# One block per chunk in the DeltaNet matrices, and a second pair of heads that runs two steps behind

## The reference

```
gcum = cumsum(g);  decay = exp(gcum_i - gcum_j) where i >= j, else 0
a_mat = where(i > j, (k*beta) @ k^T * decay, 0) + I          # 64 x 64
u, w  = solve(a_mat, [v*beta, k*beta*exp(gcum)])             # unit lower triangular
v_new = u - w @ state
o     = (q*exp(gcum)) @ state + ((q @ k^T) * decay) @ v_new
state = state*exp(gcum_end) + (k*exp(gcum_end - gcum))^T @ v_new
```

## Time and profile before

| | us |
|---|---|
| median of 3 runs | 2914.16 |
| these runs | 2910.6, 2914.16, 2915.44 |
| profiled execution's own time | 2922.2 |
| its span, first to last instruction | 2920.4 |

### The profile page before, as it was taken

One profiled execution on the slowest core, in us unless ns is written; L12 is line 12 of the kernel. 1 busy time (PEld: TensorE's weight loads), 2 busy tenths in 40 slices (PEclk: granted clock), 3 DMA queues, 4 the chain that ended last, 5 costly groups with the idle time before them and its releaser, 6 DMA issues.

```text
span 2920.4 us, 37357 instructions
## 1 busy us (share of the span) xinstructions
PE 2310.8 (79%) x12376; PEld 1057.1 (36%) x12376; DVE 2092.9 (72%) x5401; ACT 1428.7 (49%) x4102; POOL 1178.7 (40%) x1032
## 2 busy tenths in 40 slices
PE   9998888787978888788786678667786677678887
PEld 5465433243422443234432333223332333233332
DVE  3857877777777776777766777777766777776664
ACT  4425545564456455454443544444444544444344
POOL 0003444444444434444444444444444444444442
PEclk9999989999988889899987898988988899989999
DMA  7348999999999999999999999999999999999998
GB/s 269 104 168 355 418 410 409 415 411 419 419 419 420 410 389 372 419 420 416 405 406 421 418 416 416 413 421 416 412 404 421 420 416 412 414 421 421 421 421 349
DMA packets 187042, 1148.16 MB, mean 393 GB/s; under 512 B 19808, under 2 KB 40288, under 8 KB 55648
## 3 DMA queue, kind: packets, MB, share of 16 engines
q0 software_dynamic: 147456, 1073.81, 89.2%
q1 hardware_dynamic: 24512, 53.67, 5.1%
q10 hardware_dynamic: 14880, 18.29, 1.7%
HBM read 1132.06 MB, written 13.63 MB: 392 GB/s over the span
## 4 chain that ended last, share of the span: by engine, by line
DMA 38%; PE 32%; DVE 11%; ACT 7%; issue 3%; POOL 3%; ACTq 0%; DVEq 0%; POOLq 0%
DMA ring_mem<-in_experts,work 37%; PE bank L1985 13%; DVE ring_mem L1607 6%; PE bank L1842 4%; PE bank L1641 3%; PE bank L1966 3%; POOL ring_mem L813 3%; PE bank L1802 3%; PE bank L1891 2%; ACT work L1149 1%; DMA kept_tiles<-ring_mem 1%; ACT work L1145 1%; ACT L1145 1%; PE bank L1799 1%; ACT L984 1%
## 5 line engine op out<-in xcount | busy, mean ns | idle before, releaser
L813 POOL DMA_INDIRECT ring_mem<-in_experts,work x1024 | 1178.3, 1151 | 1717.0 <-PE bank L1986 1154.1
L1607 DVE CUSTOM_DVE_ANT_0 ring_mem<-ring_mem,work 128x1024 f32<-128x1024 f32 x1024 | 1251.9, 1223 | 554.1 <-DMA ring_mem<-in_experts,work 544.8
L1985 PE MATMUL bank<-ring_mem,work 64*64 64x512 f32 x3584 | 1022.3, 691 | 352.9 <-ACT work L1149 347.8
L1986 PE MATMUL bank<-ring_mem,work 64*64 64x512 f32 x3584 | 1022.4, 691 | 0.0
L1145 ACT ACTIVATE work<-work 128x1 f32<-128x1 f32 x1024 | 206.3, 202 | 1167.7 <-DVE work L1607 1128.9
L1985 PEld LDWEIGHTS bank<-ring_mem,work 64*64 64x64 f32 x3584 | 247.9, 147 | 885.8 <-ACT work L1149 510.0
L1149 ACT ACTIVATE work<-work 128x64 f32<-128x64 f32 (+1 forms) x1024 | 364.3, 356 | 34.0 <-ACT work L1145 0.2
L1137 ACT ACTIVATE work<-kept,work 128x64 f32<-128x64 f32 x896 | 298.5, 333 | 9.0 <-DVE work L1461 9.0
L1966 PE MATMUL bank<-ring_mem,work 128*128 128x512 f32 x512 | 249.5, 622 | 47.1 <-ACT work L1149 46.9
L1641 PE MATMUL bank<-work 128*128 128x128 f32 x1080 | 189.8, 316 | 114.5 <-ACT work L923 65.6
L1891 PE MATMUL bank<-late,work 128*128 128x256 f32 x1008 | 249.5, 391 | 2.7 <-DVE work L1367 2.3
(11 more groups left out here) (362 smaller groups left out, 2268.6 us busy)
## 6 DMA issues: line engine op xcount, KB each, us to landing
ring_mem<-in_experts,work POOLq DMA_INDIRECT x1024
work<-in_wc ACTq DMA_DIRECT2D x20, 512.0 KB
late<-in_wc SPq DMA_DIRECT2D x16, 512.0 KB, 3.8
work<-kept_tiles SPq DMA_DIRECT2D x14, 384.0 KB
x_all<-in_x SPq DMA_DIRECT2D x8, 512.0 KB, 12.0
x_all<-in_w_out SPq DMA_DIRECT2D x1, 4096.0 KB, 19.6
work<-in_x SPq DMA_DIRECT2D x8, 512.0 KB
late<-in_w_late SPq DMA_DIRECT2D x2, 1920.0 KB, 12.7
```

What stands on the lines that cost most here:

```text
L813: G.indirect_dma_start(ring[k % RING], None, a["experts"], bass.IndirectOffsetOnAxis(ap=picks[:, j * TOPK + k:j * TOPK + k + 1], axis=0)). ...
L1607: V.tensor_tensor_reduce(out=row, in0=row, in1=hf_tile[t % 2], scale=1.0, scalar=0.0, op0=ALU.mult, op1=ALU.add, accum_out=dots[:, k:k + 1 ...
L1985: PE.matmul(to[high if odd else low], of[low], row[low], start=(q == 1 and odd == 1), stop=(q == PICKS - 1))
L1986: m = PE.matmul(to[low if odd else high], of[high], row[high], start=(q == 1 and odd == 1), stop=(q == PICKS - 1))
```

## The change

It has four parts.

1. The matrices between the tokens of a chunk are held as two 64x64 blocks side by side over the partitions: 128 partitions x 64 columns per head instead of 128 x 128. The first chunk's block is on partitions 0 to 63, the second's on 64 to 127. Products of them are four 64x64 matmuls instead of two 128x128 ones; vector and scalar operations run over 128 columns for a pair instead of 256. One of them, L1244, goes; the mask is added in step 1, which becomes four operations. The transposes of step 4 become matmuls with the identity.
2. In the first tile the loop has 37 steps, and the second pair of heads runs two steps behind the first (`LAG`).
3. The grown unit of a head with number 5 in its tile (only head 5 has one) loads its weights at pick 0 instead of 2 and is projected in picks 6, 7, 8, 8 instead of 8, 9, 10, 10.
4. The small columns of head 19 are made in eight picks from pick 4 on, 4 matmuls each, instead of in four picks from pick 7 on, 8 each.

```diff
-WORK = 9888 - 1024
+WORK = 9888 - 1024 + 2 * CHUNK
...
+    low = (j < CHUNK)
+    level_c = np.where(low, level[:, :CHUNK], level[:, CHUNK:])
...
-N_MARKS = 2 * P
+N_MARKS = 2 * P + 2 * CHUNK
...
+                self.dec_c, self.inv_c, self.inv_t_c, self.solve_c, self.scores_c = (
+                    ap[:, 0:2 * CHUNK] for ap in (self.dec, self.row, self.inv_t, self.solve, self.scores))
+                self.half_c = [ap[:, 0:2 * CHUNK] for ap in self.half]
...
-        STEPS = 35
+        STEPS, LAG = 35, 2
...
         def project_at(w):
 
+            if GROWN_AT[w] % PHEADS == 5:
+                return 6, 7, 8, 8
...
@@ ACT, delta @@
-                        A.activation(at.dec, at.dec, ACT.Exp)
+                        A.activation(at.dec_c, at.dec_c, ACT.Exp)
...
-                        A.activation(at.row, at.half[0], ACT.Copy).then_inc(D["inv_made"], 1)
+                        A.activation(at.inv_c, at.half_c[0], ACT.Copy).then_inc(D["inv_made"], 1)
...
-                        A.activation(at.dec, at.half[1], ACT.Copy).then_inc(D["prod_kept"], 1)
+                        A.activation(at.dec_c, at.half_c[1], ACT.Copy).then_inc(D["prod_kept"], 1)
...
-                        A.activation(at.k_sum, at.half[5], ACT.Copy).then_inc(D["uw_kept"], 1)
+                        A.activation(pair(at.k_sum)[:, :, low], pair(at.half_c[5]), ACT.Copy)
+                        A.activation(pair(at.k_sum)[:, :, high], pair(at.half_c[2]), ACT.Copy).then_inc(D["uw_kept"], 1)
...
-                    if k == 2 and load_late(w):
+                    if k == (0 if GROWN_AT[w] % PHEADS == 5 else 2) and load_late(w):
...
@@ ACT, DVE and PE @@
-                for s in range(STEPS):
-                    delta(s, 0)
-                    delta(s, 1)
+                for s in range(STEPS + LAG):
+                    if s < STEPS:
+                        delta(s, 0)
+                    if s >= LAG:
+                        delta(s - LAG, 1)
...
@@ DVE, delta @@
-                            m = V.tensor_scalar(at.dec[:, cols], at.half[0][:, cols], log_sum[:, first + h:first + h + 1], 0.0, ALU.subtract, ALU.min)
+                            for of in (low, high):
+                                m = V.scalar_tensor_tensor(at.dec_c[of, h * CHUNK:(h + 1) * CHUNK], at.half[0][of, h * P + of.start:h * P + of.stop],
+                                                           log_sum[of, first + h:first + h + 1], not_causal_c[of], ALU.subtract, ALU.add)
...
-                        vc.link(V.scalar_tensor_tensor(pair(at.dec), causal_only, 0.0, pair(at.dec), ALU.is_gt, ALU.mult))
...
-                            V.tensor_tensor(at.row, at.row, at.half[2], ALU.subtract).then_inc(D["inv_done"], 1)
-                        V.tensor_tensor(at.inv_t, at.inv_t, at.half[3], ALU.subtract).then_inc(D["level_done"], 1)
+                            V.tensor_tensor(at.inv_c, at.inv_c, at.half_c[2], ALU.subtract).then_inc(D["inv_done"], 1)
+                        V.tensor_tensor(at.inv_t_c, at.inv_t_c, at.half_c[3], ALU.subtract).then_inc(D["level_done"], 1)
...
@@ PE @@
+                def blocks_of_two(to, left, right):
+
+                    for h in range(2):
+                        c = slice(h * CHUNK, (h + 1) * CHUNK)
+                        for of in (low, high):
+                            m = PE.matmul(to[of, c], left[of, c], right[of, c], start=True, stop=True)
+                    return m
+
+                def gram(to, left, right):
+
+                    for h in range(2):
+                        for of in (low, high):
+                            m = PE.matmul(to[of, h * CHUNK:(h + 1) * CHUNK], left[:, h, of], right[:, h, of], start=True, stop=True)
+                    return m
...
-                            m = PE.transpose(at.half[0][:, c], at.inv_t[:, c], ident)
+                            for of in (low, high):
+                                m = PE.matmul(at.half_c[0][of, c], at.inv_t_c[of, c], pair_ident[of], start=True, stop=True)
...
-                        two(at.half[1], at.dec, at.row).then_inc(D["prod_made"], 1)
+                        blocks_of_two(at.half_c[1], at.dec_c, at.inv_c).then_inc(D["prod_made"], 1)
...
-                            two(at.half[2], at.inv_t, at.dec)
-                        two(at.half[3], at.dec, at.inv_t).then_inc(D["corr_made"], 1)
+                            blocks_of_two(at.half_c[2], at.inv_t_c, at.dec_c)
+                        blocks_of_two(at.half_c[3], at.dec_c, at.inv_t_c).then_inc(D["corr_made"], 1)
...
-                        two(at.half[4], at.inv_t, at.v_kept)
-                        two(at.half[5], at.k_sum, at.inv_t).then_inc(D["uw_made"], 1)
+                        for h in range(2):
+                            c, wide = slice(h * CHUNK, (h + 1) * CHUNK), slice(h * P, (h + 1) * P)
+                            for of in (low, high):
+                                PE.matmul(at.half[4][of, wide], at.inv_t_c[of, c], at.v_kept[of, wide], start=True, stop=True)
+                                m = PE.matmul(at.half_c[5 if of is low else 2][:, c], at.k_sum[of, wide], at.inv_t_c[of, c], start=True, stop=True)
+                        m.then_inc(D["uw_made"], 1)
...
-                                m = PE.matmul(at.half[2][:, cols], at.scores[:, cols], at.dec[:, cols], start=False, stop=True)
+                                for of in (low, high):
+                                    m = PE.matmul(at.half[2][of, cols], at.scores_c[of, h * CHUNK:(h + 1) * CHUNK], at.dec[of, cols], start=False, stop=True)
...
@@ PE, small_columns @@
-                    if head == SMALL_HEAD and 7 <= k < 7 + PASS:
-                        if k == 7:
+                    if head == SMALL_HEAD and 4 <= k < 4 + 2 * PASS:
+                        if k == 4:
...
-                        t = k - 7
-                        for d in range(DB):
+                        t, part = (k - 4) // 2, (k - 4) % 2
+                        for d in range(part * 4, part * 4 + 4):
```

More of the change, by code:

```diff
@@ L108, in constants @@
         level = level + (n + 1) * ((j // (2 * s) == i // (2 * s)) & (j % (2 * s) < s) & (i % (2 * s) >= s))
-    cols = [j == i, np.broadcast_to(np.arange(TOPK), (P, TOPK)), (j % CHUNK) == i[:, :CHUNK], np.ones((P, P)), level, same & (j <= i), same & (j > i)]
+    low = (j < CHUNK)
+    level_c = np.where(low, level[:, :CHUNK], level[:, CHUNK:])
+    cols = [j == i, np.broadcast_to(np.arange(TOPK), (P, TOPK)), (j % CHUNK) == i[:, :CHUNK], np.ones((P, P)), level, level_c,
+            np.where(level_c > 0, 0.0, LOW), same & (j <= i), same & (j > i)]
     for w in POOL_WINDOWS:
@@ L174, in build @@
         marks = lasting(N_MARKS)
-        ones, level = marks[:, 0:P], marks[:, P:]
+        ones, level, level_c, not_causal_c = marks[:, 0:P], marks[:, P:2 * P], marks[:, 2 * P:2 * P + CHUNK], marks[:, 2 * P + CHUNK:]
         log_dec, log_sum, beta, sum_dec, dec_end = (lasting(TH) for _ in range(5))
@@ L670, in over_pair @@
         def over_pair(ap):
-            return ap.unsqueeze(1).to_broadcast([P, 2, P])
+            return ap.unsqueeze(1).to_broadcast([P, 2, ap.shape[1]])
         def raw(u, kind):
@@ L1247, in delta @@
                             dve.wait_ge(D["gated_turned"], u)
-                        vc.link(by_beta(at.solve, at.half[2], at.dec, first))
-                        vc.link(V.scalar_tensor_tensor(pair(at.inv_t), causal_only, 1.0, pair(at.solve), ALU.is_equal, ALU.mult))
-                        V.tensor_tensor(pair(at.inv_t), over_pair(ident), pair(at.inv_t), ALU.subtract).then_inc(D["inv_t_made"], 1)
+                        vc.link(by_beta(at.solve_c, at.half_c[2], at.dec_c, first))
+                        vc.link(V.scalar_tensor_tensor(pair(at.inv_t_c), over_pair(level_c), 1.0, pair(at.solve_c), ALU.is_equal, ALU.mult))
+                        V.tensor_tensor(pair(at.inv_t_c), over_pair(pair_ident), pair(at.inv_t_c), ALU.subtract).then_inc(D["inv_t_made"], 1)
                     elif s == 4:
@@ L1254, in delta @@
                         V.tensor_tensor(pair(at.q_dec), raw(u, 0), pair(at.row), ALU.mult).then_inc(D["queries_made"], 1)
-                        vc.mark(by_beta(at.scores, at.half[3], at.dec, first))
+                        vc.mark(by_beta(at.scores_c, at.half_c[3], at.dec_c, first))
                     elif s == 5:
@@ L1308, in lower @@
                     at = place(u)
-                    V.scalar_tensor_tensor(pair(at.dec), over_pair(level), float(n + 2), pair(at.solve), ALU.is_equal, ALU.mult).then_inc(D["lower_made"], 1)
+                    V.scalar_tensor_tensor(pair(at.dec_c), over_pair(level_c), float(n + 2), pair(at.solve_c), ALU.is_equal, ALU.mult).then_inc(D["lower_made"], 1)
                 def pool_step(g, i):
@@ L1657, in delta @@
                         k = raw(u, 1)
-                        for h in range(2):
-                            PE.matmul(at.half[2][:, h * P:(h + 1) * P], k[:, h, :], k[:, h, :], start=True, stop=True)
```

(4 more changed lines are left out.)

7 lines of the change are left out of this document (3 added, 4 removed).

## The result

The changed kernel takes 2926.16 us (median of 7 runs, 2923.47 to 2929.92) against 2914.33 (7 runs, 2910.6 to 2919.71) for the kernel before. The record gives a ratio of 1.0037, 95% interval 1.0028 to 1.0047 (the two medians divided give 1.0041). The forecast was 2907.5, its range 2899 to 2918.

A forecast was written before the change was run, and what follows sets the result against it. Gathers of expert rows filling the DMA engines were taken as the bound, so only the first loop and DMA holes could pay. The loop's -2.8 and the holes' -3.8 made -6.6 us, giving 2907.5 us, range 2899 to 2918.

The forecast's parts named there:

- (a): First tile's DeltaNet loop up to the end of step 11: 21.8 us instead of 24.0, a win of 2.2.
- (b): First tile's loop, steps 12 to 21: 12.7 us instead of 16.15, a win of 3.4.
- (c): First tile's loop, step 22 to the end of the products: 15.1 us new, including work moved there by the lag.
- (d): Tail of the first loop behind the second pair's output: 2.5 us stand bare instead of 0.3.
- uw of the first pair 1.2: Step 20 in the first loop: the first pair's u and w products would stream in 1.2 us.
- 1.1 in (c): The second pair's u and w products, falling later in the first loop through the lag: 1.1 us more.
- visit: TensorE going from whole array to blocks and back: 0.30 us of change, 0.52 with one product; low end 0.16.
- rival (3): Less PE work in the pick slots drops the clock to 1.2 GHz and opens new holes: 2920 us, chance 0.10.
- 3.2 us of waits: TensorE's waits in steps 12 to 21 of the first loop, for ACT copies and uw to ws: about 3.2 us.
- rival (2): Blocks sharing one PSUM bank run one behind the other, making the first loop 5.8 us longer: 2918 us, chance 0.10.
- Four weight products: Weight products in steps 12 to 21 of the first loop: 1.78 us of TensorE streaming.
- The holes: Gaps in DMA traffic behind the first gather, near 505, 635, 970, 1060, 2090 us: -3.8 us, bounds 0 and -9.

The follow-up runs named there:

- the grouped kernel: Changed kernel, lag still 2, with step 20's matmuls ordered by shape, all u then all w: 2916.11 us, ratio 1.000; repeated, 2915.06 us, 0.9997.
- the last kernel: Changed kernel with step 20 ordered by shape and a lag of 0, without the edits for head 5 and the small columns: 2907.87 us, ratio 0.9977.
- lag 3: Changed kernel with step 20 ordered by shape and the second pair three steps behind instead of two: 2918.28 us, ratio 1.0008.
- The late edits: Kernel before with only head 5 projected two picks earlier and the small columns over eight picks: 2915.21 us, ratio 0.9997.
- the filled kernel: Changed kernel, alternating step 20 and lag 2 kept, with about 4.4 us of unused extra TensorE products in steps 15 to 19: 2927.31 us, ratio 1.0045.

## Why the prediction was wrong

Its parts (a) to (d), forecast against measured, in us. The marks in the changed kernel are 148.23, 170.65, 191.29 (191.85 less the wait of 0.56), 212.44 (211.58 and two passes of 0.43) and 214.65:

| part | forecast | changed kernel | off by |
|---|---|---|---|
| (a) to the end of step 11 | 21.8 | 22.4 | +0.6 |
| (b) to the first pair's step 21 | 12.7 | 20.6 | +7.9 |
| (c) to the last pool-out product | 15.1 | 21.2 | +6.1 |
| (d) bare tail | 2.5 | 2.2 | -0.3 |
| loop | 52.2 | 66.4 | +14.2 |

Against the kernel before the loop's 11.3 us are three things: the blocks, grouped and without a lag, -2.6 (52.4 against 55.1, the wait for z included); the lag of two steps, +4.7 (57.1); the alternating order with the clock that it brings down, +9.3 (66.4). With no lag that order costs 4.9 only (57.4 against 52.4), so the two losses feed each other.

**The step that failed is "uw of the first pair 1.2" in (b), and the same 1.1 in (c).** It took step 20 for one visit to the blocks, with one change of shape. But the diff writes u and w of each block one behind the other, and the two have different tiles (64x64 and 64x128): eight groups of two passes, with a change between each. The price of such a change stood in the rows used: the two column blocks of L1716 and L1717 in front of a whole-array product cost 0.16 us above their streaming, and the text even took 0.16 as the low end of a "visit". Two passes of 128 columns stream 0.21 us (those of w stand for as much, as the grouped kernel shows), so 0.36 a group is 0.15 of change, as in that row; and two blocks that would overlap no longer follow each other. (The Trainium skill has this in words: "Changing tiling mode (not just tile) drains the TensorE", in "TensorEngine Tiling (Array Packing)", Key Properties; it gives no price, and the trace agrees with 0.15 to 0.16 us a change.) At full clock this is 2.9 us for 1.2, twice: 3.4 us. The runs show it, since grouping gives 1.18. By estimate 0.9 of the 1.7 us of one step 20 are its six changes more, and the rest is overlap lost.

**The clock** was rival (3), but in the wrong place: it was looked for behind the gather, in picks with little work, not in a loop where rows 3 gave a granted clock of 1.00. The two stretches at 1.2 GHz cost, over the same work at 2.4 GHz, 1.5 (step 20), 0.9 (L1896) and 0.6 (L1654, one L1662 visit) in (b), and 3.2 in (c): 6.2 us. Together with the 3.4 that is 9.6, against the 9.3 by which the grouped kernel's loop is shorter (66.42 less 57.09), whose wait ahead of the second pair's step 20 is 0.3 longer. So this one oversight is worth 9 to 10 of the 14.2 us.

**The lag.** The text said that with the lag PE has the other pair's products to do in the wait for L923, and yet put 3.2 us of waits into (b), more than the 1.24 of the kernel before. They were 3.5, so the term was right; what it did not ask is what a lag of 0 would have with the same blocks: 1.3. What had looked like PE waiting for ACT's L923 behind `keep_weights` with nothing else to do was, as the runs with a lag suggest, one wait that served both pairs. With a lag each pair has its own, in an in-order stream. The lag costs 4.7 us in blocks (57.1 less 52.4) and some 5 in the whole-array form. The tail's part in this was overrated: the text has 2.5 us stand bare "instead of 0.3", but its own 3.4 less 2.6 leaves 0.8, and 0.94 was measured before, so the lag adds 1.3 and not 2.2 (the sum of the loop is not touched by this, rival (2)'s is). In blocks the grouped kernels have 2.2 bare at a lag of 2, and at a lag of 0 2.2 and 1.4, because of z.

**Mis-sized terms.** Four weight products were put at 1.78; they are eight passes of 0.11 each, 0.89, so 3.56 in all (as one look at "x8" in the timeline of before would have told): +1.8. The waits of (b) +0.3, the 0.56 us ahead of the second pair's step 20 in (c) was not forecast. The rest of (b) and (c) is some 1.7 us. A part of it is the visits (next paragraph), eight in (b) at 0.05 us too little; the others were not traced further.

**What was right.** Blocks that share a PSUM bank overlap: from start to next start a visit takes 0.38 us with one product, 0.61 with two and 0.85 with three. That looks less than the 0.52, 0.73 and 0.95 of the text, but theirs include what the neighbours pay: L1886 between two visits takes 1.06 us to the next start (158.50 to 159.56) and not 0.86. So a visit costs 0.57, 0.80 and 1.04, with 0.36 us of change and not 0.30: the upper of the text's two values. Rival (2), and with it what the Trainium skill says in "TensorEngine Tiling (Array Packing)", Gotcha 1, does not hold here: L1662's two row blocks write one bank, and eight passes of 64 columns take 0.38 us to the next start with the change of shape, where their streaming one behind the other alone is 0.43. (a) is right to 0.6 us, about what its twelve visits at 0.05 too little make; the tail is right to 0.3, the hole at 505 is gone.

**The holes** were put at -3.8 us. Comparing each run's time with its loop (time won or lost against before, less the same for the loop with the stretch near 150 taken off) gives, with the times by the ratios, between -3.3 (the last kernel) and +0.7 us (lag 3), -1.4 in the mean of the nine with blocks (with the times by the medians -4.9 to +0.5, -1.7 in the mean); each is uncertain by about 3 us, and whether the kernel before has the stretch near 150 in its other executions isn't known. A gain of the forecast's sign, perhaps a third of its size; it stays open. The late edits are worth nothing within the 3 us that their interval leaves.

## What to carry to other kernels

Count changes of tile shape, not visits: products in blocks of several shapes go shape by shape, so that blocks on different rows or columns stand next to each other; the same matmuls in alternating order cost two and a half times as much (2.88 us for 1.18) and can take the clock down for several us behind them. Before two chains are staggered on an in-order engine to hide a wait, ask whether they share that wait now: if so, the stagger splits one wait into two. And a change of several parts should be priced against each part alone: here the blocks, grouped, are worth 5 to 8 us of gain by themselves, and the lag and one order of matmuls turned this into a loss of 12.

## What the runs showed of the hardware

- A pair of 64-row passes that alternates between a 64-column and a 128-column tile costs 0.36 us at 2.4 GHz and 0.61 at 1.2 GHz, whether its passes stream 128 columns or 64 (L1725 and L1726). Eight passes of one shape, on two blocks of rows, cost 0.58 to 0.60 at 2.4 GHz.
- In small tile products in such an order TensorE went to the 1.2 GHz level even where its records are without a gap: in each of the three alternating kernels looked at above the granted clock fell during a step 20, earliest where waits stood before it (184.2, after two groups of the first pair), later with fewer waits or more work before it (185.5 after twelve groups; 197 after fourteen in the filled kernel), and never there in the six grouped runs, among them two whose waits before it are the same. So neither an unbroken row of records nor a busy share of 2.00 of 2.00 us says that the clock will stay; the granted clock of the window has to be read.
- Near 150 us, behind a wait of 2.57 us for DVE, seven of the twelve profiles have a stretch at 1.2 GHz of about 3 us, the others none, the kernel before and the changed one among those. It costs 1.56 us, and its cause is not in what the kernels differ by: of the two runs of the grouped kernel one had it. Here it starts in the grouped kernel, L1889 taking 1.30 to the next start where the changed kernel's L1886 took 1.05:

```profile
149.23 1.36 PE L1889 MATMUL bank<-ring_mem,late 128*128 128x512 f32 x2
150.53 0.70 PE L1669 MATMUL bank<-late 128*64 128x64 f32 x8
```

It must be taken off before loops of single profiles are compared.
